# Sums of squares for four norms: six pairs of matmuls against six element-wise passes on VectorE and one pair

## The reference, cut to what matters

```python
def rms_norm(x, w):
    x32 = x.astype(jnp.float32)
    y = x32 * lax.rsqrt(jnp.mean(x32 * x32, axis=-1, keepdims=True) + EPS)
    return (y * w.astype(jnp.float32)).astype(x.dtype)
...
    for i in range(DEPTH_2):
        pre, post, mix, ffn = layers[i]
        mixer = griffin_swa_mixer if i % 2 == 0 else mamba2_mixer
        h = h + rms_norm(mixer(rms_norm(h, pre), *mix), post)
        f_pre, f_post, w_up, c_w, c_b, w_down = ffn
        h = h + rms_norm(conv_ffn(rms_norm(h, f_pre), w_up, c_w, c_b, w_down), f_post)
```

## Time and profile before

| | us |
|---|---|
| Median of 3 runs | 3109.65 (3108.88 to 3119.19) |
| The profiled execution, its own time | 3110.36 |
| Its span, from first to last instruction | 3108.5 |
| PE busy | 2854.5 (92%) |
| DVE busy | 1035.6 (33%) |
| ACT busy | 620.8 (20%) |
| POOL busy | 268.8 (9%) |
| Mean granted clock of PE | 0.940 |

### The profile page before, as it was taken

One profiled execution on the slowest core, in us unless ns is written; L12 is line 12 of the kernel. 1 busy time (PEld: TensorE's weight loads), 2 busy tenths in 40 slices (PEclk: granted clock), 3 DMA queues, 4 the chain that ended last, 5 costly groups with the idle time before them and its releaser, 6 DMA issues.

```text
span 3108.5 us, 37906 instructions
## 1 busy us (share of the span) xinstructions
PE 2854.5 (92%) x14859; PEld 2136.6 (69%) x14859; DVE 1035.6 (33%) x2148; ACT 620.8 (20%) x1304; POOL 268.8 (9%) x368
## 2 busy tenths in 40 slices
PE   4999887678994999999999999999989899999998
PEld 2554683423332886687888788888877687888787
DVE  6355642311114342604333201113437604333202
ACT  1121220101112453602111001111127402111000
POOL 3121220011220000000000000000006400000000
PEclk7999998689997998999999999999978899999999
DMA  5133102478963111011212122122210011212122
GB/s 226 69 123 122 55 1 122 160 293 356 377 246 126 68 67 56 2 68 55 79 70 73 62 108 108 60 76 68 81 41 2 1 68 58 78 67 81 54 109 81
DMA packets 49449, 312.15 MB, mean 100 GB/s; under 512 B 12192, under 2 KB 14496, under 8 KB 18336
## 3 DMA queue, kind: packets, MB, share of 16 engines
q1 hardware_dynamic: 39520, 290.28, 24.5%
q0 software_dynamic: 9216, 17.85, 1.5%
q10 hardware_dynamic: 576, 2.10, 0.2%
HBM read 351.08 MB, written 16.78 MB: 118 GB/s over the span
## 4 chain that ended last, share of the span: by engine, by line
PE 65%; DVE 2%; ACT 1%; issue 0%; DVEq 0%; POOL 0%; POOLq 0%; ACTq 0%
PE ps L489 35%; PE ps L1001 18%; PE ps L1044 2%; PE ps L966 1%; PE ps L1168 1%; PE ps L984 1%; PE ps L952 1%; PE ps L1140 1%; PE ps L1163 1%; PE ps L991 1%; PE ps L1176 0%; PE ps L1195 0%; PE ps L897 0%; PE ps L1166 0%; PE ps L1118 0%
## 5 line engine op out<-in xcount | busy, mean ns | idle before, releaser
L489 PE MATMUL ps<-u,ring 128*128 128x264 f32 (+1 forms) x5248 | 1253.6, 401 | 27.4 <-DVE u L1675 20.7
L489 PEld LDWEIGHTS ps<-u,ring 128*128 128x128 f32 x5248 | 998.9, 191 | 272.5 <-issue 97.5
L1001 PE MATMUL ps<-work,ring 128*128 128x264 f32 x2432 | 557.6, 389 | 10.8 <-DVE work L1678 8.9
L1001 PEld LDWEIGHTS ps<-work,ring 128*128 128x128 f32 x2432 | 466.4, 192 | 93.5 <-DVE work L1678 9.7
L1675 DVE TENSOR_SCALAR work<-tmp,par 128x528 f32<-128x528 f32 (+2 forms) x136 | 74.9, 551 | 663.6 <-ACT tmp L1578 335.7
L1681 DVE SCALAR_TENSOR_TENSOR work<-tmp,par,work 128x528 f32<-128x528 f32 (+2 forms) x320 | 245.5, 767 | 50.0 <-issue 46.4
L829 PE MATMUL ps<-work,u 128*64 128x512 f32 x640 | 175.4, 615 | 32.3 <-DMA work<-in_experts,rs 30.1
L2285 DVE RECIPROCAL rs<-rs 128x264 f32<-128x264 f32 x8 | 14.4, 1803 | 529.7 <-ACT rs L1520 529.0
L1678 DVE TENSOR_TENSOR work<-work 128x128 f32<-128x128 f32 (+7 forms) x366 | 141.6, 425 | 62.2 <-ACT work L1450 18.4
L1578 ACT ACTIVATE tmp<-ps 128x528 f32<-128x528 f32 x80 | 48.9, 612 | 499.6 <-PE ps L489 499.6
L829 PEld LDWEIGHTS ps<-work,u 128*64 128x64 f32 x640 | 56.7, 142 | 109.5 <-issue 106.6
(11 more groups left out here) (355 smaller groups left out, 2811.5 us busy)
## 6 DMA issues: line engine op xcount, KB each, us to landing
ring<-in_stream SPq DMA_DIRECT2D x169, 1024.0 KB, 4.8
work<-in_experts SPq DMA_DIRECT2D x25, 2048.0 KB, 14.5
work<-in_experts SPq DMA_DIRECT2D x25, 1024.0 KB, 9.3
ring<-in_experts SPq DMA_DIRECT2D x7, 2048.0 KB, 12.6
ring<-in_experts SPq DMA_DIRECT2D x7, 1024.0 KB, 8.7
work<-rows_out SPq DMA_DIRECT2D x4, 1024.0 KB, 8.0
h<-in_x_fm SPq DMA_DIRECT2D x1, 2048.0 KB, 10.7
rows_in<-work ACTq DMA_DIRECT2D x4, 512.0 KB, 2.6
```

What stands on the lines that cost most here:

```text
L489: m = pe.matmul(pair(q, half, cnt), ring[:, (n + b // 16) % WSLOTS, b % 16 * P:(b % 16 + 1) * P], x[:, lo:lo + cnt], start=(k == 0), stop= ...
L1001: return pe.matmul(pair(q0 + t, half, HALF), block(t, kk), rhs[kk][:, half * HALF:(half + 1) * HALF], start=(kk == 0), stop=(kk == parts - 1))
```

## The change: what it does

DVE gets six instructions at the head of each `edge`: it copies the square of tile 0 to `sq_sum`, which lies in `tmp`, and adds the squares of tiles 1 to 5 to it, one by one, each after `squares_ready`. Each gives `squares_added`, on which ACT now waits before it overwrites a buffer of `sq` (tiles 2 to 7), instead of on `squares_used`. PE drops `both_sums` and runs one pair of matmuls over `sq_sum`, where the pair of tile 5 stood; it gives `squares_used` a step of 6, so that the later counts stay as they were. The sums of tiles 6 and 7 and all later ones are untouched.

```diff
+ADDED = lambda n: FULL * EDGE[n]
...
+        sq_sum = tmp[:, 0, 3:T2 + 3]
...
-            def both_sums(i, first):
-
-                pe.wait_ge(sem("squares_ready"), i + 1)
-                for half in range(2):
-                    m = pe.matmul(ps[:, 6 + half, 0:HALF], ones, sq[:, i % 2, half * HALF:(half + 1) * HALF],
-                                  start=first, stop=False)
-                m.then_inc(sem("squares_used"), 1)
-
...
                     m.then_inc(sem("tile_done"), 1)
-                    if t:
-                        both_sums(i0 + t - 1, t == 1)
                 for t in (FULL, FULL + 1):
...
                     if t == FULL:
-                        both_sums(i0 + FULL - 1, False)
+                        pe.wait_ge(sem("squares_added"), ADDED(n) + FULL)
+                        for half in range(2):
+                            s = pe.matmul(ps[:, 6 + half, 0:HALF], ones, sq_sum[:, half * HALF:(half + 1) * HALF],
+                                          start=True, stop=False)
+                        s.then_inc(sem("squares_used"), FULL)
...
                 def square(i, src, cols):
-                    act.wait_ge(sem("squares_used"), i - 1)
+                    if i < i0 + DT:
+                        act.wait_ge(sem("squares_added"), ADDED(n) + i - i0 - 1)
+                    else:
+                        act.wait_ge(sem("squares_used"), i - 1)
...
-                    act.wait_ge(sem("squares_used"), i0 + t - 1)
+                    if t < 2:
+                        act.wait_ge(sem("squares_used"), i0 + t - 1)
+                    else:
+                        act.wait_ge(sem("squares_added"), ADDED(n) + t - 1)
...
             def edge(n, src, gain, next_gain):
 
+                for t in range(FULL):
+                    i = EDGE_SQ(n) + t
+                    dve.wait_ge(sem("squares_ready"), i + 1)
+                    if t == 0:
+                        m = dve.tensor_copy(sq_sum, sq[:, i % 2, :])
+                    else:
+                        m = tt(sq_sum, sq_sum, sq[:, i % 2, :], add)
+                    m.then_inc(sem("squares_added"), 1)
+                    dve.drain()
```

## The result

| | before | after |
|---|---|---|
| Median of 5 runs, us | 3110.89 (3108.88 to 3119.19) | 3095.74 (3084.99 to 3096.15) |
| Ratio, with 95% interval | | 0.9936 (0.9914 to 0.9957) |
| Profiled execution, its own time | 3110.36 | 3096.15 |
| Its span | 3108.5 | 3094.3 |

The change makes the kernel 0.4 to 0.9% faster. In a second set of runs, with its own runs of the kernel before, the ratio was 0.9938 (0.9924 to 0.9952). Both intervals hold the 0.9943 that 17.8 us would be. The medians differ by 15.15 us in the first set and by 18.59 in the second (3089.49 against 3108.08). The predicted 3091.9 lies between the medians of the changed kernel in the two sets, 3095.74 and 3089.49.

A forecast was written before the change was run, and what follows sets the result against it. The prediction took PE's own instructions to bound the products. -17.8 us for 20 pairs, with 0 for DVE, wait and clock, gave 3091.9 us against 3109.65 (-0.57%), range 3086.5 to 3097.7.

The forecast's parts named there:

- What bounds the products: In `out0` and `down0` PE's own instructions set the time: the chain stays on PE unbroken, busy 76.50 and 103.20 us.
- The price of a pair from the chain, not from the record or a rule: A pair of sums takes 0.89 us of PE's chain; 20 pairs removed give 17.8 us, 4.45 in each product.
- DVE's adds at nothing: Six DVE instructions per product, 4.1 us each product, 16.4 in all, hidden where DVE idles; cost 0.
- The wait at nothing: PE's wait for the sixth `squares_added` after half 0 of tile 6 costs 0; 5.3 and 8 us to spare.
- Rival 2: Between tiles 6 and 7 PE waits for a late sum; 8 us go and the time is 3100; chance 0.03.
- The clock at nothing, with 3 us to either side: Low-clock loss after PE idles, behind the first removed pair, was taken as unchanged: 0, some 3 us either way.
- the six stretches: Stretches after PE's idling, behind the first removed pair, losing 13.0 us before; the sum was to stay near that.
- Rival 1: The clock takes back 2.3 to 5.8 us in stretches after PE's idling: 3094.2 to 3097.7 us; chance 0.13.
- "faster": Whole kernel below 3094.1 us, a gain of 15.5 us or more; chance 0.77.
- The range: Whole kernel between 3086.5 and 3097.7 us.
- Rival 3: In the products loads or PSUM reads replace the sums as the limit; nothing gained, 3109.7 us; chance 0.04.
- rival 4: Three stretches of 48 records after the reciprocals run wholly at 1.2 GHz: +26.6 us, time 3118.5; chance 0.03.

The follow-up runs named there:

- DVE's part alone: DVE's copy and adds put into the kernel before, result unused, PE's pairs kept, ACT waiting for both readers of a square: ratio 0.9998 to before.
- POOL's sums: Changed kernel, with POOL also adding the eight squares of `h` for half 0 of the next norm in three of four products: ratio 0.9944 to before.

## Why the prediction was right

- **What bounds the products.** Right, and shown from both sides: PE's removed pairs give 4.45 us in `out0`, doubled ones cost 5.34, each pair 0.89. The reciprocals of half 0 were to come 4.45, 8.9, 13.35 and 17.8 us earlier, but for the clock: counted from the start of `out0` it is 4.45, 9.03, 11.60 and 16.42 us in the first profile after and 4.44, 8.70, 13.54 and 20.24 in the second.
- **The price of a pair from the chain, not from the record or a rule.** Right. Four records of 386 ns would have been 1.54 us a pair, 30.9 in all; 112 ns a matmul, which the prediction works out by the table in "VectorE: DVE Perf Modes" of the Trainium skill, would have given 4.5 us in all. Both are outside both intervals.
- **DVE's adds at nothing.** Right; DVE's part alone leaves every stage as it was. The add took 708 ns as its row said. The copy took 435 ns where 555 had been taken, within the bounds.
- **The wait at nothing.** Right: the cover left is 5.6 us (5.3 predicted), and without it the price is 1.71 us a product (1.8 predicted). Rival 2 is excluded.
- **The clock at nothing, with 3 us to either side.** For what it counted this held: the six stretches lose 12.8 and 12.1 us in the two profiles after, against 13.0. But two more places of the same kind were left out. The 34 records behind the first reciprocal of `pre_norm` took 1.7 us more in one profile, and the way from `in2` to `out2` 1.6 us less in the other. The whole came to 1.4 us taken back and 2.5 us given, so the sum of 0 within 3 stands, in part by luck. That the losses differ between executions, which no row before could show, these two profiles of one program do. And the prediction took low clock to follow idling alone, while the head of the scan has it with PE busy (see the last section).
- **Rival 1** (the clock takes part back) needed 2.3 us more in the six stretches and is excluded by the profiles, not by the totals. Its times, 3094.2 to 3097.7, hold the first median, 3095.74. The prediction's own line for "faster", a gain of 15.5 us, is missed by the first set (15.15) and passed by the second (18.59). With executions this far apart the 0.77 for "faster" against 0.13 for rival 1 was more than totals could decide.
- **The range.** Ahead of `out0`, where nothing was edited, twelve profiles reach it between 1306.90 and 1316.01 us, and the prediction did not count that at all. Eleven timed executions of the changed kernel lie between 3082.70 and 3096.15 us, a spread of 13.5 us, wider than the predicted range of 11.2. The mechanism puts the centre where it was predicted; that a median of five, 2.0 us from the upper end, still fell inside the range was also luck.
- **Rival 3** (PE is not the limit: the gain would have been nothing) and **rival 4** (low clock throughout) did not occur; the dearest stretch of 48 records seen in any run took 13.92 us, and rival 4 needed 21.4.

## What to carry to other kernels

Where the chain stays on one engine without a break, an instruction taken out of it is worth the distance to the next one's start, and the work may go to an engine that waits there, even the one that paces the norm, as long as its own slack in that place is larger than what is added. Compare a stage's duration from profile to profile: here it showed 0.45 us exactly, while whole executions scattered by 13. An idle engine is not free if its instructions lengthen those of the engine that sets the pace, as POOL's adds did to DVE's.

## What the runs showed of the hardware that was not expected

- The low-clock losses after idling can repeat exactly, and can differ for one and the same program. DVE's part alone began `out0` 2.28 us earlier than the profile of before, yet its stretches have the same durations. Its three of 48 records, in the chain of waits, read as follows; the earlier trace rows have 13.91, 10.95 and 12.63. The changed kernel, profiled twice, had 10.95, 12.64 and 13.88 us once and 12.63, 12.63 and 10.95 the other time.

```profile
1455.87 13.92 PE ps L1046 x48
...
1954.81 10.95 PE ps L1046 x48
...
2617.85 12.63 PE ps L1046 x48
```

- In all runs such a stretch took from 10.95 to 13.92 us. What selects the combination these runs do not show.
- Low clock does not need idling. Before, PE passes from a dense stretch at a granted clock of 1.00 (2275.0 to 2288.4 us, busy throughout) to 80 records of 128x32 (L1118), 12.11 us busy out of 12.20. The clock is 1.00 in their first 2.6 us and 0.50, the level of 1.2 GHz, from 2294.0 on; 0.71 over the whole. The same 80 records took 12.08 us before, 11.60 and 11.30 in the two profiles after, and 14.27 with POOL's sums.
- POOL and DVE slow each other on float32 adds of 264 elements: 433 to 561 ns (TENSOR_TENSOR) and 488 to 605 ns (SCALAR_TENSOR_TENSOR) in the mean on DVE, 650 to 890 ns for single ones on POOL.
